# The second layer's input projection as two products of seven blocks, on one Trainium2 core

## What is computed

```python
for i in range(DEPTH):                      # DEPTH = 2
    h = _rmsnorm(x, g_pre[i])
    o = _even_mixer(h, ...) if i % 2 == 0 else _odd_mixer(h, ...)
    x = x + _rmsnorm(o, g_post[i])
    x = x + jax.nn.sigmoid(x @ w_ple_gate[i]) * (p[i] @ w_ple[i])

def _odd_mixer(h, w_in, q_norm_g, kv_norm_g, w_uq, w_ukv, w_out):
    z = h @ w_in                            # 1024 -> 1952 columns
    c_q, c_kv, k_rope, g_c, f_in, g_d = _split(z, ODD_SPLITS)   # 256, 128, 32, 512, 512, 512
    q = _rmsnorm(c_q, q_norm_g) @ w_uq      # latents: normed, rotated, turned
    kv = _rmsnorm(c_kv, kv_norm_g) @ w_ukv
    ...
    c_out = _mla_attention(...) * jax.nn.silu(g_c)
    f = jnp.fft.fft2(f_in ...).real
    d_out = f * jax.nn.silu(g_d)
    return jnp.concatenate([c_out, d_out], axis=-1) @ w_out
```

## Time and profile before

| | |
|---|---|
| time, median of 3 runs | 1911.21 us (1910.17 to 1915.01) |
| profiled execution | 1912.66 us, its span 1910.9 us |
| mean granted clock of TensorE | 0.995 of full speed |
| PE busy | 1864.0 us, 98% of the span, 9712 matmuls |
| DVE busy | 1208.3 us, 63% |
| ACT busy | 733.2 us, 38% |
| POOL busy | 790.7 us, 41% |

### The profile page before, as it was taken

One profiled execution on the slowest core, in us unless ns is written; L12 is line 12 of the kernel. 1 busy time (PEld: TensorE's weight loads), 2 busy tenths in 40 slices (PEclk: granted clock), 3 DMA queues, 4 the chain that ended last, 5 costly groups with the idle time before them and its releaser, 6 DMA issues. The chain is left out here.

```text
span 1910.9 us, 26374 instructions
## 1 busy us (share of the span) xinstructions
PE 1864.0 (98%) x9712; PEld 1580.7 (83%) x9712; DVE 1208.3 (63%) x1823; ACT 733.2 (38%) x1475; POOL 790.7 (41%) x540
## 2 busy tenths in 40 slices
PE   6999999999999999999999999999999999999999
PEld 5888888887899788788878888887899998788887
DVE  5599999936788217523765100175777776788886
ACT  6211212211588332212223111132678787445432
POOL 2221121232687544454543231123788875354211
...
GB/s 201 45 23 84 142 83 99 144 168 108 172 288 227 198 169 215 204 119 141 130 72 24 84 94 73 85 362 168 172 144 188 197 187 284 244 177 273 272 141 141
DMA packets 145189, 302.91 MB, mean 159 GB/s; under 512 B 31601, under 2 KB 60017, under 8 KB 145074
## 3 DMA queue, kind: packets, MB, share of 16 engines
...
...
## 5 line engine op out<-in xcount | busy, mean ns | idle before, releaser
L589 DVE SCALAR_TENSOR_TENSOR ie_acc<-ie_u,ie_wconv,ie_acc 128x1551 f32<-128x1551 f32 x120 | 250.9, 2091 | 3.1
L188 POOL TENSOR_TENSOR w_lo_part<-w_raw,w_hi_part 128x1024 fp32r<-128x1024 f32 x28 | 79.3, 2837 | 346.1 <-ACT w_hi_part L180 346.1
L3073 PE MATMUL og_ps<-w_hi_part,bl_ring 128*128 128x512 f32 x672 | 216.6, 393 | 1.0 <-DVE bl_ring L2606 1.0
L242 PE MATMUL ie_ps<-rows_hi,w_hi_part 128*128 128x512 f32 x384 | 150.9, 393 | 0.0
L242 PE MATMUL ie_ps<-rows_hi,w_lo_part 128*128 128x512 f32 x384 | 149.7, 390 | 0.0
L242 PE MATMUL ie_ps<-rows_lo,w_hi_part 128*128 128x512 f32 x384 | 149.6, 390 | 0.0
L3073 PEld LDWEIGHTS og_ps<-w_hi_part,bl_ring 128*128 128x128 f32 x672 | 126.2, 188 | 26.8 <-DVE bl_ring L2606 1.1
L3073 PE MATMUL og_ps<-w_lo_part,bl_ring 128*128 128x512 f32 x336 | 130.8, 389 | 0.0
L2493 DVE TENSOR_TENSOR mla_pt_lo<-mla_ps_t,mla_pt_hi 128x512 fp32r<-128x512 f32 x160 | 108.9, 686 | 33.1 <-ACT mla_pt_hi L2462 31.9
L1882 DVE SCALAR_TENSOR_TENSOR io_stage<-io_tanh,io_ps 128x512 f32<-128x512 f32 x24 | 16.5, 688 | 171.8 <-ACT io_tanh L1840 171.8
L170 POOL TENSOR_TENSOR w_hi_part<-w_raw,zero 128x1024 fp32r<-128x1024 f32 x36 | 69.4, 1927 | 127.7 <-DMA w_raw<-wall 125.4
...
## 6 DMA issues: line engine op xcount, KB each, us to landing
w_raw<-wall SPq DMA_DIRECT2D x66, 512.0 KB, 4.5
w_hi_part<-weight_blocks SPq DMA_DIRECT2D x28, 512.0 KB, 4.9
w_lo_part<-weight_blocks SPq DMA_DIRECT2D x28, 512.0 KB, 5.7
weight_blocks<-w_hi_part SPq DMA_DIRECT2D x26, 512.0 KB, 6.2
w_flat<-wall SPq DMA_DIRECT2D x16, 512.0 KB, 8.8
weight_blocks<-w_lo_part SPq DMA_DIRECT2D x16, 512.0 KB, 5.1
weight_blocks<-w_raw_rounded SPq DMA_DIRECT2D x14, 512.0 KB, 5.9
op_in<-x SPq DMA_DIRECT2D x12, 512.0 KB, 4.5
```

Of the source, the lines that this page charges most:

```text
L188: pool.tensor_tensor(g.W[1][:, pair % 2, off:off + QCOLS], g.raw[:, n % 2, :], g.W[0][:, pair % 2, off:off + QCOLS].bitcast(F32), ALU.subt ...
L242: mm = pe.matmul(psum[:, u % banks], w_at(g, name, a, k * HALF + c * P, P), g.XT[m][:, k, b * 512:(b + 1) * 512], start=i == 0, stop=i == ...
L589: dve.scalar_tensor_tensor(acc[:], ubuf[:, cc, s:s + CW], wconv[:, cc, s:s + 1], acc[:], ALU.mult, ALU.add).then_inc(taps, 1)
L3073: mm = pe.matmul(ps[:, N % 4], bl.part(a, N)[:, k], wb.at(N // HT, m, k), start=k + a + m == 0, stop=k == 3 and a == 1)
```

## The change

**In `in_odd`** the 48 units become two products of 2x2 blocks, each done with 7 block products instead of 8. Rows and the inner dimension are halved (A11, A12, A21, A22; 6 tiles of 128 tokens by 4 chunks), and so are the weights: B11, B21 are one pair and B12, B22 the other. Group 1 is lat and gc (lat padded to 512 columns), 7 blocks of 6 units of 12 matmuls with 512 columns. Group 2 is f and gd, 7 blocks of 8 units of 12 matmuls, four units with 512 and four with 256 columns. That makes 840 matmuls of 512 and 336 of 256 columns; before they are 864 of 512 and 288 of 480.

- The rows of h stay in fp32 (`copy_h`). DVE makes their sums S3 and S2, POOL S4 and S1. Each block's six tiles are split into a ring of six entries: ACT the high part (L1823), DVE the low part (L1827), five entries ahead of PE at most. The first three are split in `gate0` already.
- There are four PSUM banks instead of five. ACT copies the first block's product to an accumulator u (L2150); of all others DVE adds the bank to an accumulator or, where an output is complete, into the stage (L2176 to L2188). Block 1 gives one output per unit, block 5 two, block 6 one. Tanh (L2097) and sums of squares (L2090) now read the stage, and ACT does them for unit N-1 ahead of its entry for step N; in DVE's program stand, for a step, the low part of an entry, the gate product of the unit before (L2228), the latents of the one before that (L2197 to L2203), a sum, and then the bank.
- The latents are stored to DRAM, reloaded and turned late, in units 77 to 81 and 90 to 96 (`TURN_AT`).
- The stage takes 28 weight quarters instead of 16, whose high parts ACT makes and whose low parts POOL makes.
- Two of the last three turns of h come behind the first two units of `in_odd`.

**In `in_even`** POOL makes the sums of the weights' blocks that both groups need (T1 to T4), in 8 slices. A slice is two loads of 512 KB, four additions of 128x512 (L1862, L1864, L1869, L1871) in the raw ring, and one store of 1 MB (L1877). SP issues the loads at the units in `SUM_LOADS`. The slices 0 to 2 stand between POOL's weight quarters; slices 3 to 6 in its rows for the tiles t = 0 and 1, 3 and 4, 6 and 7, 9 and 10; slice 7 behind `mix(9)` and ahead of `mix(11)`. `natten`'s weight loads wait for the stores.

What is left of the diff is the moving of SBUF areas, the clearing of semaphores at other places and the new names of the weights in DRAM. The diff, cut to its core:

```diff
@@ in_even
+    LOAD_AT = {"u0": (6, 6, 8, 9), "k": (0, 0, 2, 3), "ga": (0, 0, 2, 3)}
+    SUM_LOADS = [2, 54, 66, 69, 72, 75, 78, 81]
...
         na.first_table(pool)
         for t in range(NT):
+            for x in range(3, os.SLICES):
+                if SUM_LOADS[x] + 1 == Y0 + t:
+                    os.first_sums(pool, x)
+                if SUM_LOADS[x] + 2 == Y0 + t:
+                    os.second_sums(pool, x)
             pool.wait_ge(stats, 2 * (t + 1))
             rms_scale(pool, g, mv[:, t % 2, 1:2], 1, pooled, 2 * t)
             if t >= 2:
                 mix(t - 2)
+            if t == NT - 1:
+                os.first_sums(pool, os.SLICES - 1)
         mix(NT - 2)
+        os.second_sums(pool, os.SLICES - 1)
         mix(NT - 1)
...
+class OddSums:
+    def load(self, sp, s, w_ready):
+        group, k = divmod(s, 4)
+        sp.wait_ge(self.g.w_ready, w_ready)
+        if s:
+            sp.wait_ge(self.stored, 16 * s)
+        for c in range(2):
...
+            sp.dma_start(self.g.raw_tiles[:, c:c + 3:2], src).then_inc(self.raw_in, 16)
+    def first_sums(self, pool, s):
+        pool.wait_ge(self.raw_in, 32 * (s + 1))
+        pool.tensor_tensor(b22, b22, b12, ALU.subtract).then_inc(self.summed, 1)
+        pool.wait_ge(self.summed, 4 * s + 1)
+        pool.tensor_tensor(b12, b12, b11, ALU.subtract).then_inc(self.summed, 1)
+    def second_sums(self, pool, s):
+        pool.tensor_tensor(b11, b22, b11, ALU.add).then_inc(self.summed, 1)
...
+        pool.tensor_tensor(b21, b21, b11, ALU.subtract).then_inc(self.summed, 1)
...
@@ class OddRows
+    def high(self, act, e):
+        if self.slot_used(e):
+            act.wait_ge(self.mm, self.slot_used(e))
+        act.copy(self.part(0, e), self.source(e)).then_inc(self.hi, 1)
+    def low(self, dve, e):
+        dve.wait_ge(self.hi, e + 1)
+        dve.tensor_tensor(self.part(1, e), self.source(e), self.part(0, e).bitcast(F32), ALU.subtract).then_inc(self.lo, 1)
...
@@ in_odd
-    ps = st.enter_context(nc.psum_tensor("io_ps", [P, 5, HALF], F32))
+    ps = st.enter_context(nc.psum_tensor("io_ps", [P, 4, HALF], F32))
...
+    OUTS = {1: ("C11",), 5: ("C22", "C12"), 6: ("C21",)}
...
@@ in_odd, ACT
+        for N in range(ODD_UNITS + 1):
+            if N < 2:
+                g.copy_h(act, NT - 2 + N)
+            if N >= 1:
+                for o in outs_of(N - 1):
+                    if is_gate(o) or is_lat(o):
+                        act.wait_ge(taken, total_count(o))
+                    if is_gate(o):
+                        tanh(o)
+                    elif is_lat(o):
+                        squares(o)
...
+            if N >= 3:
+                entries()
...
@@ in_odd, DVE
+        for N in range(ODD_UNITS + 2):
...
+            for e in entries_at.get(N, ()):
+                od.low(dve, e)
+            if N >= 1:
+                for o in outs_of(N - 1) if N - 1 < ODD_UNITS else ():
+                    if is_gate(o):
+                        i, x = gate_number(o), at_stage(o)
+                        dve.wait_ge(tanhed, i + 1)
+                        dve.scalar_tensor_tensor(x, th[:, i % 2, 0:x.shape[-1]], 1.0, x, ALU.add, ALU.mult).then_inc(gated, 1)
+            if N >= 2:
+                for o in outs_of(N - 2):
+                    if is_lat(o):
+                        latent(o)
...
+                if 4 <= N < 4 + HT:
+                    sum_s2(N - 4)
+                consume(N)
...
@@ in_odd, PE
+        for N in range(ODD_UNITS):
...
+            bank_free(N)
+            if group == 0:
+                pe.wait_ge(od.lo, N + 1)
+            elif x % 4 == 0:
+                pe.wait_ge(od.lo, ODD_G1 + HT * i + (6 if x else 4))
...
+            if N < 2:
+                g.turn_h(pe, NT - 2 + N)
+            if N in TURN_AT:
+                turn(TURN_AT[N])
```

More of the change, by code:

```diff
@@ L1658, in _ @@
                     h_row(u - NT - 1)
[L1659 to L1660 removed]
+                if 0 <= u - U + 3 < FIRST_ENTRIES:
+                    od.low(dve, u - U + 3)
         @g.cur.tensor
         def _(pe):
[L1664 removed]
+            for u in range(U):
                 c, t = u // NT, u % NT
```

597 lines of the change are left out of this document (421 added, 176 removed).

## The result

The changed kernel takes 1965.63 us (median of 4 runs, 1965.4 to 1966.93) against 1911.22 us: 1.0282 times the time before, with a 95% interval of 1.0265 to 1.03. The direction was forecast (+1.1%), the size was not: 54 us were lost where 20 were expected, and the time lies above the range.

A forecast was written before the change was run, and what follows sets the result against it. PE, busy 98% of the span, was taken as the bound. 1912.66 - 36 (in_odd's work) + 29 (in_odd's stalls) + 26.5 (weight sums) + 1 (clock) = 1933.2 us profiled, 1931.7 us as median; range 1900 to 1943.

The forecast's parts named there:

- the tail has no room: in_even's tail: POOL and DVE form a gapless chain, 6.63 us a tile; DVE's wait grows from 1.55 to 4.1 us.
- The seam: Entry to in_odd: 4.4 us of PE idle before the last turns of h goes, covered by twelve matmuls per wait.
- PE's own work: in_odd: matmuls and turns sum to 236.2 us against 272.3 us, so -36.0 us if nothing waits.
- PE's idle in `in_odd`: in_odd: stalls add 29 us, including 7.8 in block 1 and 13.8 around blocks 3, 5 and 6.
- The turns: in_odd, block 5: ACT and DVE take turns, 4.85 us a unit for 2.71 us of PE.
- POOL's hold on DVE: in_odd: POOL's weight quarters shut DVE out while they run; idle is 29 us with it, 20 without.
- The slices 0 to 2 are hidden: in_even before the tail: these weight sums cost nothing, as POOL is at 2 to 3 tenths there.
- The first pair: in_even's tail, tile 0: additions wait for slice 3's data, +9.3 us, of which 1 is caught up.
- Each pair adds in full, 15.5 us,: in_even's tail: six pairs of POOL additions, 2.58 us each, lengthen the chain by 15.5 us.
- The end: End of in_even's tail: slice 7's two pairs cost 5.2 us, of which the weighing gives 1.5 back.
- The clock, "+1 us": Whole kernel: one fall goes at the seam, two idles can each bring one, some 2 us each; +1 us.
- The one on the slow side (1948 us): Rival, in_odd: stalls of 42 us instead of 29, clock falls at each stall (+3 us); 1948 us, chance 0.12.

The follow-up runs named there:

- e13_no_sums_no_lows_entries_first: Changed kernel without weight sums; in in_odd, ACT casts entries ahead of tanh and squares, and POOL's low parts are on one column: 1881.78 us, ratio 0.9834.

## Why the prediction was wrong

The forecast failed at two steps. It took the weight sums' cost as POOL's additions and one late load, 26.5 us, and they cost 43.8; and it priced the clock at 1 us, where the same products kept PE busy for 12 us more in `in_odd`.

**What held.** That the tail has no room: the distances of two tiles' L652 are 6.61 and 6.64 us without a pair of additions and 9.21 to 9.24 with one whose data are there; DVE's wait is 4.14 us, forecast 4.1. The seam lost its idle. PE's own work, 236.2 us, is 3.4 us below the 239.6 busy us of `e13_no_sums_no_lows_entries_first`. PE's idle in `in_odd`, 32.2 us against 29, is close to the units that were named (10 to 16, 38 to 50, 90), and in its parts as well: 9.9 us at units 12 to 20, which wait for banks behind block 1 (forecast 7.8), 14.2 at 37 to 42 (13.8), 4.9 at 90 (3.8). The turns are real, and were over-priced at 4.85 us: 4.30, since DVE's operations in a row are 0.60 us apart. POOL's hold on DVE is real too, but the forecast's row for it, L1873, has one SBUF tensor and a scalar per partition; for two SBUF tensors it is the row of L2197 above (2.36 us) that shows it.

**What failed, up to `out_proj`** (43.8 us for 26.5). Four terms:
- *"The slices 0 to 2 are hidden"* is wrong of slice 0. The argument was POOL's idle time. But its additions ran beside DVE's scaling of the first rows, for which PE waited: PE's wait there grew from 1.45 to 5.47 us. The rows of PE, DVE and POOL:

```profile
42.34 1.94 PE L693 MATMUL ie_ps_n<-ident,w_flat 128*128 128x128 f32 x8 [5.47 <-DVE rows_lo L577]
```

```profile
34.12 6.81 DVE L572 TENSOR_SCALAR w_flat<-w_flat,ie_ss 128x1024 f32<-128x1024 f32 x4 [1.17 <-POOL ie_ss L219]
```

```profile
35.43 1.61 POOL L1864 TENSOR_TENSOR w_raw_tiles<-w_raw_tiles 128x512 f32<-128x512 f32 x1
```

  Before, the same four operations of DVE (L539) took 2.74 us. Cost 4.2 us; the hold had been used for `in_odd` and not here.
- *The first pair*, +9.3 of which 1 was to be caught up, was 10.0 (14.2 less these 4.2, by subtraction; no run has the one without the other): the term was right in kind and short by 1.7 us.
- *Each pair adds in full, 15.5 us,* is right for the additions, but from tile 0 to tile 11 it was 22.1 us. The store-and-load chain was priced for slice 3 alone; slices 5 and 6 waited as well, 4.5 and 1.2 us, and tile 1's pair, called hidden, cost 0.8.
- *The end*: 5.2 less 1.5 was forecast, and from tile 11 to `out_proj` it is 7.5 us (43.8 less 36.3). `natten`'s loads stand behind slice 7's store, and the granted clock was 0.74 and 0.69 of full speed in its first two stretches of 15 us. From `natten`'s first score to `out_proj` PE was busy for 134.5 us, where it was 127.5 before with the same products: 7 us of the clock here too, which the forecast's 1 us doesn't hold. In the tail itself the clock fell as well (0.91 from 417.9 to 530.4 us), but the tiles without a pair are 6.61 to 6.64 us apart as before, so the chain and not the clock set the pace there.

**What failed in `in_odd`** (+10.8 for -7). *The clock, "+1 us".* I allowed one or two falls of 2 us each. There were four spells at the lower level, with the stalls that end at 1053, 1062, 1152 and 1265 us; windows inside them (1052.7 to 1056.0, 1063.0 to 1066.2, 1148.3 to 1158.4, 1264.4 to 1271.0) show 0.50. PE is busy for 251.3 us where the same products took 239.6 at full clock: the mis-sized term is 12 us. One spell, behind the stall of 8.56 us at unit 42 (matmuls 0.43 us apart where 0.23 is usual, until 1158.35):

```profile
1152.66 1.19 PE L2279 MATMUL io_ps<-io_moving,w_hi_part 128*128 128x512 f32 x2 [8.56 <-issue]
1153.66 0.63 PE L2279 MATMUL io_ps<-io_moving,w_lo_part 128*128 128x512 f32 x1
1154.08 1.05 PE L2279 MATMUL io_ps<-io_moving,w_hi_part 128*128 128x512 f32 x2
...
1159.34 0.39 PE L2279 MATMUL io_ps<-io_moving,w_lo_part 128*128 128x512 f32 x1
```

The rest is 3 us of idle and 3 of PE's own work. The working put 9 us on POOL's hold (29 with it, 20 without). In idle time it was 15 (32.2 to 17.3), and in the stage 23: PE was busy for 8 us less with the same products, so spells at half clock went with the stalls.

**The rivals.** None of them happened. The one on the slow side (1948 us) named the right thing, falls of the clock at each stall, and gave it 3 us; its other part, 13 us more of idle in `in_odd`, didn't come. The forecast treated the two stages as a sum of idle times, and so did its range: neither end had a case in which late data and clock come on top.
